# Mixture-of-experts block on one core: other kinds of experts in another order, and the combine regrouped by rows of the array

## The reference

```
logits = x2d @ w_router + b_router            # 32 experts
top_v, top_i = top_k(logits, 4)
gates = softmax(top_v)
for each expert e, over its tokens:
    h = x @ w_gate_up[e] + b_gate_up[e]       # 1024 -> 2048
    h = min(h_even, 7) * sigmoid(1.702 * ...) * (clip(h_odd, -7, 7) + 1)
    out = h @ w_down[e] + b_down[e]           # 1024 -> 1024
y[token] += gate * out
```

## Time and profile before

| | |
|---|---|
| timed runs | 1248.7 us median of 3 (1247.48 to 1251.04) |
| profiled execution, its own time | 1238.82 us |
| its span | 1237.0 us |
| PE busy | 1121.9 us (91%) |
| PE weight loads busy | 480.3 us (39%) |
| DVE, ACT busy | 410.1 us (33%), 203.3 us (16%) |
| DMA, hardware queue of the weights | 422.23 MB, 83.4% of 16 engines' span |
| granted TensorE clock, mean over the span | 0.951 |

### The profile page before, as it was taken

One profiled execution on the slowest core, in us unless ns is written; L12 is line 12 of the kernel. 1 busy time (PEld: TensorE's weight loads), 2 busy tenths in 40 slices (PEclk: granted clock), 3 DMA queues, 4 the chain that ended last, 5 costly groups with the idle time before them and its releaser, 6 DMA issues.

```text
span 1237.0 us, 17034 instructions
## 1 busy us (share of the span) xinstructions
PE 1121.9 (91%) x6413; PEld 480.3 (39%) x6413; DVE 410.1 (33%) x878; ACT 203.3 (16%) x429; POOL 2.7 (0%) x6
## 2 busy tenths in 40 slices
PE   7877889999988998899898998899999999999997
PEld 5656767332332233333333233333333333333332
DVE  6888424413022121213121301333333332222223
ACT  3294322111011010011001101111111111111111
POOL 0000000000000000000000000000000000000000
PEclk9967899999799997999799979999999999999999
DMA  9412056899899986999799978999999999999980
GB/s 345 141 39 74 1 195 285 330 421 421 358 369 419 421 344 273 421 421 391 304 388 420 415 310 356 422 420 422 420 422 422 421 422 421 422 422 422 422 374 39
DMA packets 62382, 425.40 MB, mean 344 GB/s; under 512 B 8148, under 2 KB 9812, under 8 KB 12272
## 3 DMA queue, kind: packets, MB, share of 16 engines
q1 hardware_dynamic: 60544, 422.23, 83.4%
q10 hardware_dynamic: 1728, 2.11, 0.5%
q0 software_dynamic: 48, 0.15, 0.0%
HBM read 419.86 MB, written 2.51 MB: 341 GB/s over the span
## 4 chain that ended last, share of the span: by engine, by line
PE 84%; DVE 10%; issue 3%; ACT 3%; ACTq 1%; DVEq 0%
PE banks L468 79%; DVE xT L1758 2%; DVE raw L1712 1%; PE banks L765 1%; PE banks L803 1%; ACT gath L1163 1%; PE banks L841 1%; DVE hl L1724 1%; PE banks L810 0%; ACT raw_s L1207 0%; DVE G_rot L1459 0%; PE banks L848 0%; DVE Tz L375 0%; DVE hT_s L1751 0%; DVE hT L1729 0%
## 5 line engine op out<-in xcount | busy, mean ns | idle before, releaser
L468 PE MATMUL banks<-gu_ring,xe 128*64 128x512 f32 x1472 | 336.5, 600 | 0.7 <-ACT xe L1168 0.7
L1758 DVE TENSOR_TENSOR xT<-xT,banks 128x576 f32<-128x576 f32 x132 | 94.5, 752 | 514.4 <-PE banks L468 514.4
L468 PEld LDWEIGHTS banks<-gu_ring,xe 128*64 128x64 f32 x1472 | 99.3, 137 | 201.0 <-issue 197.6
L468 PE MATMUL banks<-dn_ring,hT 128*64 128x512 f32 x736 | 167.1, 601 | 10.0 <-ACT xe_s L1197 7.5
L468 PE MATMUL banks<-gu_ring,xe_s 128*32 128x512 f32 x832 | 109.2, 640 | 5.9 <-issue 5.9
L468 PEld LDWEIGHTS banks<-dn_ring,hT 128*64 128x64 f32 x736 | 50.4, 137 | 104.8 <-issue 104.1
L468 PE MATMUL banks<-gT,ye 64*128 64x288 f32 x368 | 83.9, 471 | 7.5 <-DVE xT L1758 6.9
L468 PE MATMUL banks<-x_tok,oh 96*64 96x512 f32 x288 | 69.5, 619 | 1.2 <-DVE oh L1683 1.2
L1178 ACT ACTIVATE raw<-banks 128x512 f32<-128x512 f32 x23 | 13.7, 597 | 308.3 <-PE banks L468 308.3
L468 PE MATMUL banks<-dn_ring,hT_s 128*32 128x256 f32 x832 | 50.1, 382 | 14.2 <-DVE hT_s L1751 14.2
L468 PE MATMUL banks<-gT_s,ye_s 32*128 32x288 f32 x208 | 57.5, 494 | 3.3 <-DVE xT L1758 3.3
(11 more groups left out here) (339 smaller groups left out, 886.3 us busy)
## 6 DMA issues: line engine op xcount, KB each, us to landing
gu_ring<-w_gu_dram SPq DMA_DIRECT2D x256, 1024.0 KB, 17.3
dn_ring<-w_dn_dram SPq DMA_DIRECT2D x128, 1024.0 KB, 15.3
w_out<-w_out_dram SPq DMA_DIRECT2D x2, 2048.0 KB, 8.0
w_in<-w_in_dram SPq DMA_DIRECT2D x3, 1024.0 KB, 16.0
w_in<-w_in_dram SPq DMA_DIRECT2D x4, 512.0 KB, 10.2
W<-W1c SPq DMA_DIRECT2D x16, 128.0 KB, 2.3
w_glu<-w_glu_dram SPq DMA_DIRECT2D x1, 2048.0 KB, 8.4
xT<-xT_dram SPq DMA_DIRECT2D x2, 576.0 KB, 5.6
```

The costliest lines, as they stand in the source:

```text
L468: return nc.tensor.matmul(out, lhsT, rhs, start=start, stop=stop, **kw)
L1758: X.tensor_tensor(two, two, pair[(1, 3)[c % 2]].rearrange("p (h f) -> p h f", h=2)[:, :, 0:T], ALU.add).then_inc(S("acc_done"), 1)
```

## The change

Seven edits, all in the expert part:

1. `BODY` becomes `mid, many, mid, mid`, and `KINDS` starts with two `mid`. There is no `few` any more: 28 `mid` and 4 `many`, at positions 3, 7, 11 and 15. Experts 0 and 1 stand at positions 0 and 1; the four heaviest of the others are `many`.
2. Since the order is known for positions 0 and 1, the down weights of both are loaded in `load_first` (8 chunks), ahead of the router; before, those of position 1 were loaded when the order was ready.
3. The combine works by halves. Half 0 is steps c = 0 and 2, half 1 steps c = 1 and 3. In a half of a `many`, first all four wide matmuls, then all four slim ones, in row groups q = 0, 2, 1, 3 of the array; half 1 waits for both additions of half 0. The order of steps for `mid` and for the gate bias becomes 0, 2, 1, 3, with the waits as before.
4. `down` of a `many`: wide chunks 0 and 1, slim 0, wide 2, slim 1, wide 3, slim 2, slim 3. The wait for `copied_s` stands ahead of the first slim chunk, and only if the next expert has slim slots (here never for a `many`).
5. VectorE: `accumulate` in the order 0, 2, 1, 3; `rank_at` is filled by more small copies, and one more `memset` makes the key of expert 1.
6. ScalarE: the slim tanh of a `few` stands earlier (no expert is of that kind now).
7. The loops are cut at other positions: TensorE, ScalarE and VectorE take two experts alone, then the rounds from position 2.

```diff
-BODY, ROUNDS = ("few", "many", "few", "mid"), 4
-KINDS = ["mid"] + list(BODY) * ROUNDS + ["few"] + ["mid"] * 14
+BODY, ROUNDS = ("mid", "many", "mid", "mid"), 4
+KINDS = ["mid"] * 2 + list(BODY) * ROUNDS + ["mid"] * 14
...
-        for c in range(4):
-            sp.dma_start(dn_ring[c][:], a["w_dn"][0, c]).then_inc(dn_in[c], 16)
+        for j in range(2):
+            for c in range(4):
+                sp.dma_start(dn_ring[4 * j + c][:], a["w_dn"][j, c]).then_inc(dn_in[4 * j + c], 16)
...
-        x = expert_at(0, 1)
-        for c in range(4):
-            load_dn(sp, x, c, 1)
...
+            def wide_part(c):
+                if c == 0:
+                    pe.wait_ge(S("h_ready"), w + 1)
                 pe.wait_ge(dn_in[4 * j + c], fill * 16)
...
+            def slim_part(c):
+                if c == 0:
+                    if after != "mid":
+                        pe.wait_ge(S("copied_s"), s_after * 2 + 2)
+                    pe.wait_ge(S("h_s_ready"), s + 1)
...
+            if kind == "many":
+                wide_part(0)
+                for c in range(4):
+                    if c < 3:
+                        wide_part(c + 1)
+                    slim_part(c).then_inc(S("dn_used"), 1)
+            else:
+                for c in range(4):
+                    (wide_part if kind == "mid" else slim_part)(c).then_inc(S("dn_used"), 1)
...
-            for c in range(4):
-                if c >= 2:
-                    pe.wait_ge(S("acc_done"), p * 4 + (c - 1))
-                for h in range(2):
-                    dst = pb[(2, 6)[c % 2] + h][:, 0:T]
-                    if kind != "few":
-                        rows = slice(SLOTS * h, SLOTS * h + SLOTS)
-                        last = mm(dst, ye[rows, c * P:(c + 1) * P], gT[rows], True, kind == "mid")
-                    if kind != "mid":
-                        q = 2 * h + c // 2
-                        rows = slice(FEW * q, FEW * q + FEW)
-                        last = mm(dst, ye_s[rows, (c % 2) * P:(c % 2 + 1) * P], gT_s[rows], kind == "few", True,
-                                  tile_position=(FEW * q, 0))
-                last.then_inc(S("comb_done"), 1)
+            for half in range(2):
+                if half and kind != "mid":
+                    pe.wait_ge(S("acc_done"), p * 4 + 2)
+                if kind != "few":
+                    for n in range(2):
+                        c = 2 * n + half
+                        if half and kind == "mid":
+                            pe.wait_ge(S("acc_done"), p * 4 + (n + 1))
+                        for h in range(2):
+                            rows = slice(SLOTS * h, SLOTS * h + SLOTS)
+                            last = mm(pb[(2, 6)[n] + h][:, 0:T], ye[rows, c * P:(c + 1) * P], gT[rows], True, kind == "mid")
+                        if kind == "mid":
+                            last.then_inc(S("comb_done"), 1)
+                if kind != "mid":
+                    for n in range(2):
+                        for q in (n, n + 2):
+                            rows = slice(FEW * q, FEW * q + FEW)
+                            last = mm(pb[(2, 6)[n] + q // 2][:, 0:T], ye_s[rows, half * P:(half + 1) * P], gT_s[rows],
+                                      kind == "few", True, tile_position=(FEW * q, 0))
+                        last.then_inc(S("comb_done"), 1)
...
-            link(X.tensor_scalar(extra[:], rank[:], float(N_MANY) + 0.5, None, ALU.is_lt))
-            X.tensor_scalar(key[:], rank[:], 0.5, None, ALU.is_gt)
+            link(X.tensor_scalar(extra[:], rank[:], N_MANY + 1.5, None, ALU.is_lt))
+            X.tensor_scalar(key[:], rank[:], 1.5, None, ALU.is_gt)
```

More of the change, by code:

```diff
@@ L811, in turn_hidden_s, with down @@
             last.then_inc(S("h_turned_s"), 1)
-        def down(w, s, kind, j, fill):
-            if kind != "few":
-                pe.wait_ge(S("h_ready"), w + 1)
-            for c in range(4):
+        def down(w, s, kind, after, s_after, j, fill):
+            def wide_part(c):
+                if c == 0:
+                    pe.wait_ge(S("h_ready"), w + 1)
                 pe.wait_ge(dn_in[4 * j + c], fill * 16)
-                if kind != "few":
-                    for kk in range(2):
-                        f = 2 * c + kk
-                        for h in range(2):
-                            last = mm(pb[4][SLOTS * h:SLOTS * h + SLOTS, :], hT[:, f % 4, f // 4],
-                                      dn_ring[4 * j + c][:, kk, h * HALF:(h + 1) * HALF], f == 0, f == KT - 1,
-                                      tile_position=(0, SLOTS * h))
-                if kind != "mid":
[L827 to L835, removed]
@@ new lines, in wide_part @@
+                for kk in range(2):
+                    f = 2 * c + kk
+                    for h in range(2):
+                        last = mm(pb[4][SLOTS * h:SLOTS * h + SLOTS, :], hT[:, f % 4, f // 4],
+                                  dn_ring[4 * j + c][:, kk, h * HALF:(h + 1) * HALF], f == 0, f == KT - 1,
+                                  tile_position=(0, SLOTS * h))
+                return last
+            def slim_part(c):
[3 more added lines that the diff above has]
+                    pe.wait_ge(S("h_s_ready"), s + 1)
+                if kind == "few":
+                    pe.wait_ge(dn_in[4 * j + c], fill * 16)
+                for kk in range(2):
+                    f = 2 * c + kk
+                    for q in range(4):
+                        last = mm(pb[7][FEW * q:FEW * q + FEW, 0:2 * P], hT_s[:, f % 4, f // 4],
+                                  dn_ring[4 * j + c][:, kk, q * 2 * P:(q + 1) * 2 * P], f == 0, f == KT - 1,
+                                  tile_position=(0, FEW * q))
+                return last
@@ L877, in gate_bias @@
             pe.wait_ge(S("bdnT_ready"), 2)
-            for c in range(4):
-                if c >= 2:
-                    pe.wait_ge(S("acc_done"), c - 1)
+            for n, c in enumerate((0, 2, 1, 3)):
+                if n >= 2:
+                    pe.wait_ge(S("acc_done"), n - 1)
                 for h in range(2):
                     m = 4 * h + c
-                    last = mm(pb[(2, 6)[c % 2] + h][:, 0:T], bdnT[0:NE, m * P:(m + 1) * P], gT[0:NE], True, True)
+                    last = mm(pb[(2, 6)[n % 2] + h][:, 0:T], bdnT[0:NE, m * P:(m + 1) * P], gT[0:NE], True, True)
                 last.then_inc(S("comb_done"), 1)
@@ L918, in expert @@
                 turn_gathered_s(s_after)
-            if kind != "mid" and after != "mid":
-                pe.wait_ge(S("copied_s"), s_after * 2 + 2)
-            down(w, s, kind, j, fill)
+            down(w, s, kind, after, s_after, j, fill)
         gather(0)
@@ L933, in _ @@
             for k in range(2):
-                expert(i * 2 + (19 + k), i * 2 + WIDE[19 + k], N_SLIM, "mid", "mid", "mid", (19 + k) % 2,
-                       i + ((19 + k) // 2 + 1))
-        expert(NE - 1, N_WIDE - 1, N_SLIM, "mid", "mid", "mid", 1, PAIRS)
+                expert(i * 2 + (20 + k), i * 2 + WIDE[20 + k], N_SLIM, "mid", "mid", "mid", k, i + 11)
         turn_gates(N_WIDE)
@@ L949, in _ @@
                 turn_gathered(j + (N_WIDE + 1))
-                down(j + N_WIDE, N_SLIM, "mid", 0, j + (PAIRS + 1))
+                down(j + N_WIDE, N_SLIM, "mid", "mid", N_SLIM, 0, j + (PAIRS + 1))
                 turn_gates(j + (N_WIDE + 1))
@@ L1637, in _ @@
         X.tensor_copy(iota2[:, 0], iota[:, 0:SLOTS])
[L1638 to L1642, removed]
+        r = 2
+        X.tensor_copy(rank_at[:, 0:2], iota[:, 0:2])
+        for kind in ("many", "mid", "few"):
+            at = [p for p in range(2, NE) if KINDS[p] == kind]
+            while at:
+                step = at[1] - at[0] if len(at) > 1 else 1
+                n = next((m for m in range(1, len(at)) if at[m] != at[0] + m * step), len(at))
+                X.tensor_copy(rank_at[:, at[0]:at[n - 1] + 1:step], iota[:, r:r + n])
+                at, r = at[n:], r + n
         link(X.tensor_copy(iota2[:, 1], iota[:, 0:SLOTS]))
@@ L1754, in accumulate @@
         def accumulate(b):
-            for c in range(4):
+            for n, c in enumerate((0, 2, 1, 3)):
                 two = xT[:, c::4]
-                dve.wait_ge(S("comb_done"), b * 4 + (c + 1))
-                X.tensor_tensor(two, two, pair[(1, 3)[c % 2]].rearrange("p (h f) -> p h f", h=2)[:, :, 0:T],
+                dve.wait_ge(S("comb_done"), b * 4 + (n + 1))
+                X.tensor_tensor(two, two, pair[(1, 3)[n % 2]].rearrange("p (h f) -> p h f", h=2)[:, :, 0:T],
                                 ALU.add).then_inc(S("acc_done"), 1)
@@ L1771, in _ @@
         link(X.scalar_tensor_tensor(out=key[:], in0=cnt[:], scalar=float(SLOTS), in1=ids, op0=ALU.mult, op1=ALU.subtract))
[L1772 removed]
+        X.memset(key[:, 0:1], float(SLOTS * P * P * 2))
+        link(X.memset(key[:, 1:2], float(SLOTS * P * P)))
         link(X.tensor_tensor(ahead[:], wide(key[:], 1, NE), wide(key[:], 2, NE), ALU.is_gt))
@@ L1834, in expert @@
```

(15 more changed lines are left out.)

31 lines of the change are left out of this document (15 added, 16 removed).

## The result

The changed kernel takes **1261.7 us** (median of 6 runs, 1259.18 to 1265.91); the kernel before, in the same series, 1249.87 (6 runs, 1238.23 to 1253.57). The ratio of the means is 1.011, interval 1.0065 to 1.0156: slower, by about 1%. 1271 had been forecast with a range of 1261 to 1287, so the time lies at its lower edge. From profiled execution to profiled execution it is 1238.82 to 1259.18 us, +20.4, where +22.2 was forecast. Why the two ways of comparing differ is taken up in experiment 1 and in the account of the prediction.

A forecast was written before the change was run, and what follows sets the result against it. TensorE was taken to pace the mids, with DMA 0.1 us behind. Kinds and combine +20.5 and clock +1.7 make +22.2 on the profiled execution, 1261; with the 9.9 us offset 1271 us, range 1261 to 1287.

The forecast's parts named there:

- Plain mids are TensorE's, 29.94: Plain mid windows: TensorE paces them and they stay at 29.94 us, the transfers just hidden.
- The many 43.3, the mid ahead 30.9, the mid behind 32.5, the round 136.7: Windows in a round, in us: many 43.3, mid ahead of it 30.9, mid behind it 32.5, whole round 136.7.
- The combine 5.3 with four slim matmuls in 0.7: Combine of a many on TensorE: 5.3 us in all, four slim matmuls in four row groups taking 0.7.
- A change of kind costs 0.145: Down of a many: each switch between wide and slim matmuls costs 0.145 us, two fewer save 0.29.
- No half clock behind a many: Behind each many: the old combine's 13.6 us at half clock gone; one low stretch in four rounds, +1.7 us.
- The sum +20.5 without the clock: Whole kernel: four rounds +12.7 us, position 17 and the mid behind it +6.8, expert 0 +1.0.
- The loads behind by 2.02 us at the round's start: Old rounds: DMA falls behind during the many's combine, so TensorE waits 2.02 us for weights at the next round's start.
- The offset of 9.9 us between timed and profiled: Whole kernel: timed runs of before lie 9.9 us above the profiled execution; kept for the changed kernel.
- The first rival: Timed runs: the 9.9 us are slower transfers that the new rounds don't pay, so 1262 us; chance 0.18.
- The other side: Mids: transfers, not TensorE, hold them at 29.94 us; behind a many they run faster, so 1247 us; chance 0.06.
- the one-by-one combine: Combine of a many: wide and slim matmuls still go one by one and the clock falls, 1300 us; chance 0.10.
- extra item: Expert 1: its tokens overflow its 64 slots and its weights load again, +36 us, so 1307; chance 0.04.

The follow-up runs named there:

- experiment 1: The kernel before, unchanged, timed again: 1245.32 us over 12 runs, ratio 0.9992; once more for another profile: 1255.04 us in one execution.
- experiment 6: Changed kernel with the old kinds (few, many, few, mid): 1182.68 us; then with TensorE's round loop written out: 1179.54 us; both also with half the gate/up loads.
- experiment 3: Changed kernel with combine, gate bias and accumulate put back to those of the kernel before: 1318.87 us, ratio 1.0569.
- experiment 2: Kernel before with only the new combine, gate bias and accumulate, old kinds kept: 1198.56 us, ratio 0.9615.
- experiment 4: Changed kernel with gate/up loads cut to half their columns for all experts but expert 0: 1260.69 us.

## Why the prediction was right, point by point

- **Plain mids are TensorE's, 29.94.** Right: same in the rounds, and with half the loads.
- **The many 43.3, the mid ahead 30.9, the mid behind 32.5, the round 136.7.** Measured 43.39, 30.95, 32.59, 136.87. No wait was added in `down`: slim 0 follows wide 1 without a gap.
- **The combine 5.3 with four slim matmuls in 0.7.** Measured 5.31 and 0.70. That is 3.9 times as fast as the 4 x 0.68 of one after the other in the old combine, where each stood between two wide ones. Two wide pairs took 1.17, so a pair 0.59, and against that it is 3.3 times, an estimate. The 0.89 worked out from the 3.07 of the Trainium skill (TensorE: Matmul & The Clock Gate, Packing small matmuls) was too long here.
- **A change of kind costs 0.145.** The working took 5.14 us for a mid's three chunks, where the starts give 5.31 (879.64 to 884.95), and 0.09. With two changes fewer `down` took 11.19 instead of 11.36 here, and 11.08 in experiment 6. It moves the sum by under 1 us.
- **No half clock behind a many.** Right: 1.00 through all four rounds. The one stretch of 1.7 us priced in the rounds didn't come; one of that size fell into expert 0, by luck of the same price. The prediction also missed two short stretches of the old trace, in a few and a many of the second round (clock 0.93 and 0.96); they are inside its 534.1.

```profile
383.63:407.52 23.89, 21.27 (x194) 8.49 (x194) 5.78 (x14) 3.16 (x7) 0.00 (x0) 0.93 1.01 420
407.52:452.80 45.28, 42.30 (x286) 12.87 (x285) 10.66 (x24) 3.70 (x8) 0.00 (x0) 0.96 0.92 372
```

- **The sum +20.5 without the clock.** +20.3 in span, with chance of -3.3 and +1.7 in it. Without both it is 21.9: 0.7 more than forecast in the rounds and 0.7 at the end. That it came so close is in part luck.
- **The loads behind by 2.02 us at the round's start.** Wrong. The row had said "issue", not a load; it was the loop's edge. It cost the forecast nothing, because the sum took the old rounds as they stood (534.1). But the mid at the end of a changed round pays no edge, which the sum had right only since it put 29.94 there without asking why.
- **The offset of 9.9 us between timed and profiled, kept.** This is the step that went wrong, though the time fell inside the range. It makes 7.4 of the 9 us between 1271 and 1261.7; the rest is 22.2 against 20.4. The profiled execution of before was one of its fastest, and others lose up to 15 us more, to low clock in fews and manys. The changed kernel's median lies only 2.5 us above its profiled execution. What took the scatter away is the kinds more than the combine: the new kinds with the old combine spread over 3.4 us (experiment 3, 4 runs), the old kinds with the new combine over 12.1 (experiment 2, 6 runs). The first rival had the number, 1262, but not the mechanism: it put the offset down to slower transfers.

The other side (mids paced by transfers) fell by experiment 4, the one-by-one combine by the timeline, and no extra item ran: 256 gate/up loads in the page of the profile of after. For that rival the prediction had named the Trainium skill (Perfetto Trace Analysis, Identifying the Most-Contended Engine), by which weight loads' busy share tells TensorE's headroom. That doesn't hold for a mid here: the share is 34%, matmuls are busy for 28.66 of 29.94 us, and with a third of the bytes gone it was no shorter.

## What to carry to other kernels

Price the parts of a change apart: here a regrouped combine worth 49 to 57 us and smaller edits worth 16 were delivered together with nine light experts made heavier, worth 79 us the other way, and the whole looked like a small loss. When the profiled execution is not the median one, don't carry the offset over; ask what differs between executions (mean clock beside time shows it at once) and whether the change removes it. And take "issue" in a wait at its word: in these traces a wait for weights is named as one (experiment 6), and the pauses at the loop's edge, named "issue", were none.

## What the hardware showed that I had not expected

- Where instructions were fetched anew in each round (9 fetches a round in the queue rows), TensorE's jump back cost 1.9 to 2.4 us; in the changed kernel's rounds, where no fetch recurs, it cost nothing, and the 12 mids at the end of both kernels stay at 29.94 over their loop edges. Which body size divides the two is open; only these bodies were tried.
- A DMA share of 1.01 at 421 GB/s went with a mid of 29.94 in both kernels, while a chunk landed after 19.8 us in the old and 10.6 in the new. The share doesn't tell whether anyone waits.

```profile
DMA to landing us min/median/max: 8.8/10.6/12.5
```

- In the rounds, stretches at half clock came in lengths of 3.4, 13.7 and 17.1 us and repeated from round to round of one execution, so that small differences add up: 18.0 us between the two traces of the old kernel compared above. What places them in one execution and not in another is open.
